# Memory attention beside the last column units, and the mixed rows kept plain until the output projection

## The reference

```python
h = rmsnorm(x, norm_g)
proj = h @ w_in                                  # 3200-odd columns, split among the groups
o_gla = gla_chunked(g_q, g_k, g_v, log_a)        # 4 heads, chunks of 64, a running state
o_gla = rmsnorm(o_gla, gla_norm_g) * silu(g_gate)
o_fox = fox_attention(f_q, f_k, f_v, log_f) * silu(f_gate)   # 6 heads of 64, causal, 2048 keys
mk, mv = split(rmsnorm(mem, mem_norm_g) @ w_mem_kv)          # 256 memory tokens
o_mem = softmax(m_q @ mk.T * 64 ** -0.5) @ mv * silu(m_gate) # 4 heads of 64, no mask
out = rmsnorm(x + concatenate([o_gla, o_fox, o_mem]) @ w_out, final_norm_g)
```

## Time and profile before

| | us |
|---|---|
| median of 3 runs | 1408.82 (1407.75 to 1409.83) |
| the profiled execution | 1410.44 |
| its span, first to last instruction | 1408.6 |
| TensorE busy in the span | 1281.9 (91%) |
| VectorE, ScalarE, GpSimd busy | 671.4, 547.2, 416.0 |
| granted TensorE clock, mean of the span | 0.959 of full |

### The profile page before, as it was taken

The page is one execution under the profiler, slowest core; times in us unless marked ns, Lnnn a source line. Parts: engine busy times, 40 slices in busy tenths (PEclk is TensorE's granted clock), DMA queues, the critical chain, the costliest instruction groups (busy, mean ns, idle before and its releaser), DMA issues. The chain is left out here.

```text
span 1408.6 us, 20363 instructions
## 1 busy us (share of the span) xinstructions
PE 1281.9 (91%) x6624; PEld 1038.4 (74%) x6624; DVE 671.4 (48%) x1622; ACT 547.2 (39%) x1131; POOL 416.0 (30%) x464
## 2 busy tenths in 40 slices
PE   5898999999999999999976759998999999599997
PEld 4887867888777777788854546786777777478886
DVE  4564414200545544500045547887887888322222
ACT  3563214012222222211145646776777777310100
POOL 5222431021444444430005682223223412300000
PEclk9999999999999999999977888999999999799999
DMA  6454213222544454331156535134341611465453
GB/s 212 150 156 127 76 59 114 74 82 83 157 150 153 149 157 154 125 105 64 46 150 186 133 74 137 51 112 93 89 137 29 154 24 24 146 210 193 180 205 121
DMA packets 118350, 170.40 MB, mean 121 GB/s; under 512 B 11908, under 2 KB 74628, under 8 KB 116404
## 3 DMA queue, kind: packets, MB, share of 16 engines
q1 hardware_dynamic: 115768, 160.65, 37.9%
q10 hardware_dynamic: 2304, 8.39, 1.5%
q0 software_dynamic: 192, 0.33, 0.2%
HBM read 103.19 MB, written 66.13 MB: 120 GB/s over the span
## 5 line engine op out<-in xcount | busy, mean ns | idle before, releaser
L834 PE MATMUL cg_cps<-h_T,tok_slot 128*128 128x512 f32 x2112 | 493.7, 393 | 3.4 <-POOL tok_slot L1074 3.4
L834 PEld LDWEIGHTS cg_cps<-h_T,tok_slot 128*128 128x128 f32 x2112 | 396.4, 189 | 89.2 <-POOL tok_slot L1074 4.3
L1719 PE MATMUL out_yps<-out_w,out_mix 128*128 128x512 f32 x768 | 177.4, 393 | 18.3 <-DMA out_mix<-scr_mix 17.3
L1719 PEld LDWEIGHTS out_yps<-out_w,out_mix 128*128 128x128 f32 x768 | 145.8, 190 | 49.8 <-DMA out_mix<-scr_mix 17.5
L1559 DVE TENSOR_SCALAR_CACHE_REDUCE fox_prob<-fox_sps 128x512 f32<-128x512 f32 (+2 forms) x240 | 142.1, 607 | 37.8 <-PE fox_sps L1444 34.9
L1521 ACT ACTIVATE fox_pT<-fox_tps 128x512 fp32r<-128x512 f32 x240 | 124.6, 531 | 90.1 <-PE fox_tps L1454 87.6
L1570 DVE TENSOR_TENSOR fox_pT<-fox_tps,fox_pT 128x512 fp32r<-128x512 f32 x240 | 141.7, 605 | 21.6 <-ACT fox_pT L1521 20.9
L1454 PE MATMUL fox_tps<-all_ident,fox_prob 128*128 128x128 f32 x816 | 135.1, 278 | 15.4 <-ACT fox_prob L1513 8.5
L1467 PE MATMUL fox_ops<-fox_pT,fox_v 128*128 128x512 f32 x480 | 137.3, 376 | 0.0
L1454 PEld LDWEIGHTS fox_tps<-all_ident,fox_prob 128*128 128x128 f32 x816 | 100.4, 141 | 45.5 <-ACT fox_prob L1513 11.6
L1439 PE MATMUL fox_sps<-fox_ka,fox_qa 128*128 128x512 f32 (+2 forms) x240 | 107.4, 448 | 17.4 <-PEq L1376 14.0
(11 more groups left out here) (187 smaller groups left out, 1676.3 us busy)
## 6 DMA issues: line engine op xcount, KB each, us to landing
scr_split<-cg_stage SPq DMA_DIRECT2D x64, 256.0 KB, 2.8
out_mix<-scr_mix SPq DMA_DIRECT2D x32, 512.0 KB, 4.2
tok_xin<-in_w_cols SPq DMA_DIRECT2D x22, 512.0 KB, 4.4
tok_xin<-in_x SPq DMA_DIRECT2D x16, 512.0 KB, 3.9
scr_gates<-cg_stage SPq DMA_DIRECT2D x32, 256.0 KB, 2.4
out_x<-in_x SPq DMA_DIRECT2D x16, 512.0 KB, 6.1
out<-out_o ACTq DMA_DIRECT2D x16, 512.0 KB, 5.0
scr_fox_v<-tok_vst SPq DMA_DIRECT2D x16, 384.0 KB, 2.9
```

Of the source, the lines that this page charges most:

```text
L834: mm = nc.tensor.matmul(cps[u % 2][:, :], w[j % 2][a_][:, kk, :], hT[b_][:, kk, c * CH:(c + 1) * CH], start=(kk == 0 and r == 0), stop=(kk ...
L1719: mm = nc.tensor.matmul(yps[s][:, c, :], mix[s][a][:, kk, :], w[b][:, kk, c * CH:(c + 1) * CH], start=(kk == 0 and n == 0), stop=(kk == MI ...
```

## The change

Four things are done together.

- **Memory attention moves** out of its own stage into the column stage. Turn t is spread over the units from `M0` - 2 + t: scores at unit 69 + t, transposes at 71 + t, the values at 72 + t. The 16 turns take units 69 to 87. The sums are no longer spread by matmuls: POOL multiplies the probabilities by the inverted sums before the transposes (`memory_norm`). Two heads share a tile, so that POOL gates and SP stores once for two turns (`memory_output`, `store_memory_mix`).
- **The column tiles are reordered**: raw, all gates, all split ones, with the memory queries first among the split; GLA starts at unit 34 in place of 36.
- **Mixed rows are stored plain**, one float32 array in place of two parts. The splits on POOL in the column stage and in the fox stage go, and so does the second store. The output projection loads 512 KB a tile and splits it itself: ACT copies (`mix_high`), DVE subtracts (`mix_low`), and PE waits for `mix_lo`.
- **The fox stage opens cold**: its first head is loaded at its own start, since no stage stands ahead of it that could do so.

```diff
-        self.mix = dram("scr_mix", [2, TT, P, MIX_T, P], F32)
+        self.mix = dram("scr_mix", [TT, P, MIX_T, P], F32)
...
-    KINDS = ["raw"] * NRAW + ["gate"] * 3 + ["split"] * NSPLIT + ["gate"] * (NGATE - 3)
-    FIRST_SPLIT = NRAW + 3
+    KINDS = ["raw"] * NRAW + ["gate"] * NGATE + ["split"] * NSPLIT
+    FIRST_SPLIT = NRAW + NGATE
     UNITS = NCOL * NCH
-    G0 = 36
+    G0 = 34
     STEPS = T // P
+    M0 = 71
+    TURNS = MEM_H * NCH
...
+    turns = [(2 * r + e, g) for r in range(MEM_H // 2) for g in range(NCH) for e in range(2)]
...
-                    sp.wait_ge(mix_lo, n + 1)
-                    for i in (HI, LO):
-                        sp.dma_start(scr.mix[i, n, :, 0:3, :], mst[n % 2][i][:, :, :].bitcast(F32)
-                                     ).then_inc(mix_stored[n % 2], 16)
+                    sp.wait_ge(mixed, n + 1)
+                    sp.dma_start(scr.mix[n, :, 0:3, :], mx[n % 2][:, :, :]).then_inc(mix_stored[n % 2], 16)
...
+                def load_memory(r):
+                    if r == 0:
+                        sp.wait_ge(o_done, NS)
+                        sp.wait_ge(m_filled, MEM_H)
+                        for parity in range(2):
+                            sp.wait_ge(stored[parity], CU.sent_before(NCH * (CU.FIRST_SPLIT + 2) + parity))
...
+                    if u == CU.M0 - 4:
+                        load_memory(0)
+                        load_queries(0)
+                        load_queries(1)
+                        load_memory(1)
+                    if u == CU.M0 - 3:
+                        load_memory_gate(0)
+                    t = CU.turn_at(u, -1)
+                    if t is not None and t + 2 < CU.TURNS:
+                        load_queries(t + 2)
+                    t = CU.turn_at(u, 2)
+                    if t is not None and t % 2 == 1:
+                        store_memory_mix(t // 2)
+                        if t + 1 < CU.TURNS:
+                            load_memory_gate(t // 2 + 1)
...
+                def memory_scores(t):
+                    h, g = turns[t]
+                    if t == 0:
+                        pe.wait_ge(mixed, NS)
+                    else:
+                        pe.wait_ge(m_expd, QT * t)
+                    if t % (2 * NCH) == 0:
+                        pe.wait_ge(kv_loaded[h // 2], KV_DMAS)
+                    pe.wait_ge(mq_loaded[t % 2], 32 * (t // 2 + 1))
+                    for i in range(QT):
+                        dst, queries = sps[i // 2][:, (i % 2) * M:(i % 2 + 1) * M], mq[t % 2][:, i * P:(i + 1) * P]
+                        nc.tensor.matmul(dst, queries, mka[h][:, :], start=True, stop=False)
+                        mm = nc.tensor.matmul(dst, queries, mkb[h][:, :], start=False, stop=True)
+                        if i % 2 == 1:
+                            mm.then_inc(m_scored, 1)
...
+                    t = CU.turn_at(u, 1)
+                    if t is not None:
+                        memory_weigh(t)
+                    t = CU.turn_at(u, 0)
+                    if t is not None:
+                        memory_transposes(t)
+                    t = CU.turn_at(u, -2)
+                    if t is not None:
+                        memory_scores(t)
...
+                def memory_exponentials(t):
+                    if t == 0:
+                        act.wait_ge(mixed, NS)
+                        for s in range(2):
+                            act.wait_ge(mix_stored[s], 16 * (NS // 2))
+                    for i in range(QT):
+                        if i % 2 == 0:
+                            act.wait_ge(m_maxed, 2 * t + i // 2 + 1)
+                        if t >= 2:
+                            act.wait_ge(m_transposed, MB * (t - 1))
+                        nc.scalar.activation(prob[t % 2][:, i, :], sps[i // 2][:, (i % 2) * M:(i % 2 + 1) * M], ACT.Exp,
+                                             bias=nm[t % 2][:, i:i + 1], scale=MSCALE,
+                                             accum_out=rsum[t % 2][:, i:i + 1]).then_inc(m_expd, 1)
...
+                    nc.vector.tensor_reduce(mx2[:, tiles], sps[n][:, :].rearrange("p (i c) -> p i c", c=M), AX.X, ALU.max
+                                            ).then_inc(m_reduced, 1)
+                    dve.wait_ge(m_reduced, 2 * t + n + 1)
+                    nc.vector.tensor_scalar(nm[t % 2][:, tiles], mx2[:, tiles], -MSCALE, None, ALU.mult
+                                            ).then_inc(m_maxed, 1)
...
+                    now, ahead = CU.turn_at(u, 0), CU.turn_at(u, -2)
+                    for n in range(2):
+                        if now is not None:
+                            memory_low_part(now, n)
+                        if ahead is not None:
+                            memory_maxima(ahead, n)
+                    if ahead is not None:
+                        memory_invert(ahead)
...
-                def split_mix(n):
-                    pool.wait_ge(mixed, n + 1)
-                    if n >= 2:
-                        pool.wait_ge(mix_stored[n % 2], 32 * (n // 2))
-                    nc.gpsimd.tensor_scalar(mst[n % 2][HI][:, :, :], mx[:, :, :], 1.0, 1.0, ALU.mult, ALU.mult
-                                            ).then_inc(mix_hi, 1)
-                    pool.wait_ge(mix_hi, n + 1)
-                    nc.gpsimd.tensor_tensor(mst[n % 2][LO][:, :, :], mx[:, :, :], mst[n % 2][HI][:, :, :].bitcast(F32),
-                                            ALU.subtract).then_inc(mix_lo, 1)
+                def clear_keys():
+                    pool.wait_ge(o_done, NS)
+                    pool.wait_ge(gate_ready, 3 * NS)
+                    pool.wait_ge(rstd_done, NS)
+                    for h in range(MEM_H):
+                        pool.memset(mkb[h][half(1), :].bitcast(F32), 0.0).then_inc(m_filled, 1)
+                    pool.wait_ge(m_filled, MEM_H)
+                def memory_norm(t):
+                    pool.wait_ge(m_inverted, t + 1)
+                    for i in range(QT):
+                        nc.gpsimd.tensor_scalar(prob[t % 2][:, i, :], prob[t % 2][:, i, :], rinv[t % 2][:, i:i + 1], 1.0,
+                                                ALU.mult, ALU.mult).then_inc(m_normed, 1)
+                def memory_output(n):
+                    pool.wait_ge(m_gate_loaded, 16 * (n + 1))
+                    pool.wait_ge(m_added, 2 * (n + 1))
+                    if n:
+                        pool.wait_ge(m_stored, 16 * n)
+                    nc.gpsimd.tensor_tensor(om[:, :], o[:, :], mgate[:, :], ALU.mult).then_inc(m_gated, 1)
...
-                        nc.gpsimd.tensor_tensor(o[b][:, :], o[b][:, :], gate[b][:, :], ALU.mult).then_inc(gated, 1)
-                        pool.wait_ge(gated, G.at(t + 1))
-                        pool.wait_ge(stored[b], 32 * (r * (n_turns // 2) + t // 2))
+                        pool.wait_ge(stored[b], 16 * (r * (n_turns // 2) + t // 2))
                         pool.sem_inc(pool_goes, 1)
-                        nc.gpsimd.tensor_scalar(om[b][HI][:, :], o[b][:, :], 1.0, 1.0, ALU.mult, ALU.mult).then_inc(o_hi, 1)
-                        pool.wait_ge(o_hi, G.at(t + 1))
-                        nc.gpsimd.tensor_tensor(om[b][LO][:, :], o[b][:, :], om[b][HI][:, :].bitcast(F32),
-                                                ALU.subtract).then_inc(o_lo, 1)
+                        nc.gpsimd.tensor_tensor(om[b][:, :], o[b][:, :], gate[b][:, :], ALU.mult).then_inc(gated, 1)
...
+        mix_raw = [k.sb(f"mixraw{s}", [P, MIX_T, P]) for s in range(2)]
...
-                    for i in (HI, LO):
-                        sp.dma_start(mix[s][i][:, :, :].bitcast(F32),
-                                     scr.mix[i, bass.ds(t, 1)].rearrange("a p k t -> (a p) k t")
-                                     ).then_inc(mix_loaded[s], 16)
+                    sp.dma_start(mix_raw[s][:, :, :], scr.mix[bass.ds(t, 1)].rearrange("a p k t -> (a p) k t")
+                                 ).then_inc(mix_loaded[s], 16)
                     sp.dma_start(xin[s][:, :], x_t[bass.ds(t, 1)].rearrange("a p d -> (a p) d")
                                  ).then_inc(x_loaded[s], 16)
                 load(0, 0)
+                load(1, 1)
                 for kk in range(RAW, MIX_T):
                     sp.wait_ge(w_lo, kk - RAW + 1)
                     weights.load(sp, kk)
-                load(1, 1)
                 with sp.Fori(1, TT // 2) as h:
                     for s in range(2):
                         t = 2 * h + s
-                        sp.wait_ge(projected, t - 1)
+                        sp.wait_ge(mix_lo, t - 1)
                         sp.sem_inc(sp_goes, 1)
                         sp.wait_ge(added, t - 1)
...
-                    pe.wait_ge(mix_loaded[s], 32 * (h + 1))
+                    pe.wait_ge(mix_lo, t + 1)
...
+                def mix_low(t, s):
+                    dve.wait_ge(mix_hi, t + 1)
```

(23 more changed lines are left out.)

265 lines of the change are left out of this document (202 added, 63 removed).

## The result

The changed kernel takes **1345.9 us** (median of 4 runs, 1344.0 to 1346.1), the kernel before 1409.1 (1407.8 to 1409.8). The ratio is 0.9549, 95% interval 0.9533 to 0.9566: 63 us less. The forecast was 1339, in a range of 1331 to 1358. The profiled execution took 1346.05 us with a span of 1344.3; of the 7 us, 5.1 lie in the span (forecast 1339.2), the rest between span and median.

The account below looks back on a forecast made before the run. PE was taken to bound the column stage, and no engine the memory-attention stage. The terms 1408.6 - 110.8 + 44.8 + 0.5 - 4.9 + 1.0 gave 1339.2 us of span, so a median of 1339 us, range 1331 to 1358.

Parts of the forecast that it names:

- What bounds the kernel: Column stage: PE bounds it, so 16 turns add 44.8 us of PE work, including 0.2 a turn for changes of kind.
- Whether PE waits in the turns: Units with turns: the other engines need less than the 8.2 us of a unit, so their work is hidden.
- The handover: Units 66 to 69: 22 DMAs queued on SP before unit 67's store delay PE by 0.5 us (0 to 5).
- The fox stage's entry: Last unit to first fox score: handover 4.8, fill 6.1, issue 4.6 and landing 3.3 sum to 18.8 us.
- Second and third pieces: Fox stage's opening: the second piece is just there when PE asks, later ones have more room; cost 0.
- Table loads: Column stage: ScalarE's 26 table loads in place of 5 take 27 us of ScalarE; cost 0.
- The plain rows: Fox stage's end saves 4.9 us without splits and second store; the projection's entry costs 1.0 us more.
- 1: Turns beside the units: PE waits 1 to 2 us a turn, +16 to +32, 1355 to 1371 us; chance 0.11.
- 3: Transposes in the turns cost PE 0.275 us each, their stated length: +24, 1363 us; chance 0.02.
- 4: Units: waits lower the clock; slower than before from nine of 16 units at half clock on; chance 0.02.
- 2: The two cold entries cost more, by late pieces and late tile splits: +6 to +13, 1345 to 1352; chance 0.10.
- 5: Fox stage: fewer stores and loads let it run closer to PE's 342 us, -5 to -12; chance 0.05.

Follow-up runs that it names:

- e6: The changed kernel with each of the 128 transposes of the memory probabilities done twice: 1358.7 us, ratio 0.9636 to the kernel before.
- e5: The changed kernel with each of the 64 exponentials of the memory attention computed twice on ScalarE: 1346.2 us, ratio 0.9548 to the kernel before.
- e1: The changed kernel with the second pair's keys and values loaded at unit 73's place in SP's program, not unit 67's: 1342.8 us, ratio 0.9527.
- e3: The changed kernel with the last memory output stored ahead of the last column unit's store on SP: 1344.8 us, ratio 0.9543.
- e2: The changed kernel with seven of the fox stage's first nine loads issued before SP waits for VectorE's fill: 1341.3 us, ratio 0.9518.
- e11: The changed kernel with all small edits to loads, stores and fill combined, and four early fox loads issued by ScalarE: 1333.5 us, ratio 0.9468.
- e4: The kernel before with only the plain mixed rows, split in the output projection; memory attention stays its own stage: 1392.8 us, ratio 0.9880.
- e0: The changed kernel run again without any edit: 1346.4 us, ratio 0.9555 to the kernel before.
- e9: The changed kernel with later second keys, early fox loads, last memory output stored first, second mixed tile behind weights, fill in four pieces: 1334.4 us, ratio 0.9468.

## Why the prediction was right, and where it was low

**What bounds the kernel.** Right. The stretch of units that was full of PE work stayed so, at 8.21 us for a unit with its turn (forecast 5.44 + 2.8 = 8.24). The whole of the turns came to 44.9 us (44.8). That rested on start-to-start distances of matmuls, and e6 shows the method on the transposes, whose length in the record, 0.272 us, is 2.5 times their cost of 0.11. The prediction had 0.09 for it, and its 0.2 us for the changes of kind took the difference up.

**Whether PE waits in the turns.** Right: behind the handover it doesn't, and e5 shows 2 us of ScalarE to spare and used. The scaling on POOL takes 0.48 us, for 0.5. The maxima and everything else on VectorE fit into 4.3 us a turn, for 5.0.

**The handover, 0.5 us booked.** The step failed, at 3.8 us. The 22 DMAs and the store of unit 67 behind them were in the text (12 us of issue by its reckoning, 617.71 - 603.26 = 14.5 in the trace), and it followed them to PE's unit 71, which was not late. Behind the store of unit 69 the same queue holds the queries of the third turn, and PE asks for these. The prediction's bound of 0 to 5 us held. e1 takes the second wait away by moving nine loads. The first wait, 1.0 to 1.2 us, stays there; it is for the first two turns' queries, which SP issues behind the first pair's keys and values.

**The fox stage's entry, 18.8 us.** The mechanism was right and two of four terms were small: the handover, 6.2 for 4.8, of which e3 gives 0.5 for the store of the last memory output, queued behind the last unit's, and the rest isn't explained; and the landing, 4.1 for 3.3. (The fill of 6.1 that the sum uses is 6.0 in the text's own working; it measured 6.1.) I took the landing between 2.25 us for 128 KB alone and what a busy queue might do. e2 and e11 show that the landing isn't a term by itself: it is what is left of the piece's transfer when the issues are through.

**Second and third pieces, 0.** Right for the change: no wait on a piece beyond the first. That it was thin shows in e2, where an entry 7 us shorter makes the second piece late by 1 us.

**Table loads, 0.** The column stage has 35 table loads for 14, the 21 more that the text had reckoned, and no PE wait for ScalarE's exponentials or gates stands in the columns. Not tried by itself.

**The plain rows.** At the fox stage's end 4.7 us for 4.9. In the projection's steady part no PE wait for `out_mix` but the first. At its entry +1.7 for +1.0: the waits for weights are 2.0 us for the 1.02 of the earlier trace rows, and PE starts 6.1 us after the first instruction there. What the text lacked is what the split of these rows cost in the memory stage, 11 us (e4).

**The start of the columns, and the fox stage.** +1.4 and -2.7 us between the two profiles, both booked at 0. Repetition makes most of both a matter of the execution. One profile of each kernel can't tell this; the granted clock that every run lists could have.

**The rivals.** 1 falls by the third row of windows and by e5, 3 by e6. 4 falls by its size, not by its mechanism: the granted clock is 1.00 in the third row of windows, but in e0, e3 and e5 the lower level did come into the units behind a wait of 2.0 to 2.4 us, once, for 3.4 us and a price of 1.6, where the rival needed nine units of it. 2 has a part of the miss, 2.8 us at the two entries, but not its mechanism of late pieces. 5 didn't come: the fox stage's PE work is as before, and most of its shorter time goes with the clock.

**The range.** By the bounds that the text gives (turns -4, entries -2), its lower end is 1333 and not 1331. Nothing hangs on it.

## What to carry to other kernels

Where one engine is busy without a gap, work for it is priced by start-to-start distances, and work for the others is free until it fills the period; both held within a few per cent. What was missed twice was the next entry in an in-order queue, at the handover and at the fox stage's entry: when loads are put into SP's row in a block, follow everything queued behind them until it reaches the engine that bounds the kernel, not only the first thing. And before crediting a large move with a whole stage's time, ask what in that stage a smaller edit would have removed: here 11 of 120 us.

## What the runs showed of the hardware

A load of 4 KB issued last let PE start 1.4 us after its issue, one of 256 KB behind eight others 4.1 us (e2 and the changed kernel). With a piece of 1032 KB, taking its last issue from 4.7 to 2.2 us behind the first moved PE's start by 0.4 us (e9 and e11). In these two kernels, then, the issues no longer bounded the cold loads.

The time at the lower clock level after a long wait of PE scatters: in two executions of the same kernel with the same wait of 20.8 and 20.9 us it was 4.8 us of the first 12 in one (e0, above), and 7.5 in the other (4, and by the mean of 0.78 another 3.5; the clock was full between 5 and 7 us behind the first score, and then fell again):

```profile
784.69:788.69 4.00, 4.00 (x14) 2.82 (x14) 1.95 (x10) 1.59 (x5) 0.00 (x0) 0.50 0.74 204
788.69:796.69 8.00, 6.50 (x26) 4.25 (x25) 5.12 (x20) 3.36 (x10) 0.00 (x0) 0.78 0.76 212
```

Over all profiles it was 4.7 to 12.4 us, for 358.6 to 361.5 us of the stage, longer in the main where it was longer (e5 is the exception above): a scatter the size of the small edits that were to be judged here.

Among the units, a wait of 1.96 us was enough for a fall in e0, and one of 2.61 us in the first profile was not. Each of the three falls there lasted 3.4 us and made one unit 1.6 us longer.
